# The first chunk of a gated-delta stage in another order: key transposes and two unread products first, value rows last, and the second inverse sent from another queue

## What is computed

```python
def gdn_chunk(S, xs):
    q, k, v, g, beta = xs
    ...
    a_mat = jnp.where(strict, beta[..., :, None] * jnp.einsum('bhid,bhjd->bhij', k, k) * decay, 0.0)
    lmat = a_mat + jnp.eye(c, dtype=F32)
    rhs = jnp.concatenate([beta[..., None] * v, (beta * jnp.exp(G))[..., None] * k], axis=-1)
    sol = lax.linalg.triangular_solve(lmat, rhs, left_side=True, lower=True, unit_diagonal=True)
    u, w = sol[..., :DV_A], sol[..., DV_A:]
    v_new = u - jnp.einsum('bhck,bhkv->bhcv', w, S)
    qk = jnp.einsum('bhid,bhjd->bhij', q, k) * decay
    o = jnp.einsum('bhck,bhkv->bhcv', q * jnp.exp(G)[..., None], S) + jnp.einsum('bhij,bhjv->bhiv', qk, v_new)
    ...
```

```python
def sb_sample(q, k_new, v_new, cache_k, cache_v, page_table, bias):
    ...
    return (jnp.einsum('bhqk,bkhd->bqhd', a[..., :past], vp)
            + jnp.einsum('bhqk,bkhd->bqhd', a[..., past:], v_new))
```

## Time and profile before

| | us |
|---|---|
| median of 3 runs | 1370.7 (1368.13 to 1372.23) |
| the profiled execution | 1375.66 |
| its span in the trace | 1373.6 |
| PE busy | 1321.5 (96%) |
| DVE busy | 800.4 (58%) |
| ACT busy | 524.5 (38%) |
| POOL busy | 177.4 (13%) |

### The profile page before, as it was taken

How to read it: one execution, slowest core, us unless ns; L and a number is a source line. 1 busy time by engine, 2 the same in 40 slices (tenths; PEclk the granted TensorE clock), 3 DMA queues, 4 the chain that set the end, 5 groups by cost and what they waited for, 6 DMA issues and landing times.

```text
span 1373.6 us, 27802 instructions
## 1 busy us (share of the span) xinstructions
PE 1321.5 (96%) x10527; PEld 1217.2 (89%) x10527; DVE 800.4 (58%) x2973; ACT 524.5 (38%) x794; POOL 177.4 (13%) x252
## 2 busy tenths in 40 slices
PE   6999999998999899999999999999999999999998
PEld 5999976787799787878988788999999999999998
DVE  5688759967989947886574223345544444433222
ACT  4333357635855422334325332234422222222222
POOL 1000001100720352400310000001211111110000
PEclk9999999999999969999999999999999999999999
DMA  8559968759733289989879986423333333332232
GB/s 307 175 177 321 329 205 299 262 189 333 232 100 101 67 278 331 366 293 308 240 232 344 370 280 200 139 78 92 90 94 93 92 94 92 94 88 87 85 100 74
DMA packets 256859, 265.56 MB, mean 193 GB/s; under 512 B 22987, under 2 KB 215677, under 8 KB 255927
## 3 DMA queue, kind: packets, MB, share of 16 engines
q1 hardware_dynamic: 256295, 262.75, 59.1%
q10 hardware_dynamic: 432, 1.06, 0.2%
HBM read 244.26 MB, written 19.70 MB: 192 GB/s over the span
## 4 chain that ended last, share of the span: by engine, by line
PE 70%; DVE 10%; DMA 6%; SPq 6%; ACT 4%; issue 3%; POOL 2%; POOLq 0%; ACTq 0%; DVEq 0%
PE ps L1178 51%; DMA wring<-in_w_in 3%; PE ps L1216 3%; PE ps L1290 3%; SPq L781 2%; DVE kring L2405 2%; DVE R L2486 2%; PE ps L1301 1%; DVE wring_split L646 1%; PE ps L1275 1%; PE ps L1475 1%; PE ps L1492 1%; SPq L847 1%; POOL R L3061 1%; SPq L784 1%
## 5 line engine op out<-in xcount | busy, mean ns | idle before, releaser
L1178 PE MATMUL ps<-obT_split,wring_split 128*128 128x268 f32 (+2 forms) x1296 | 263.2, 284 | 0.0
L1178 PE MATMUL ps<-obT_split,qv_split 128*128 128x260 f32 (+2 forms) x1024 | 214.1, 290 | 5.0 <-DVE wring_split L646 3.4
L646 DVE TENSOR_TENSOR wring_split<-wring,vring_split 128x1024 fp32r<-128x1024 f32 (+1 forms) x92 | 118.7, 1291 | 149.3 <-ACT vring_split L640 149.2
L1178 PEld LDWEIGHTS ps<-obT_split,wring_split 128*128 128x128 f32 (+1 forms) x1296 | 200.2, 187 | 0.5
L1178 PE MATMUL ps<-obT_split,vring_split 128*128 128x260 f32 (+1 forms) x960 | 195.8, 285 | 0.7 <-issue 0.7
L1178 PE MATMUL ps<-xn_split,vring_split 128*128 128x260 f32 (+1 forms) x960 | 193.2, 282 | 0.0
L1178 PE MATMUL ps<-xn_split,qv_split 128*128 128x260 f32 (+2 forms) x896 | 182.1, 285 | 0.0
L1178 PEld LDWEIGHTS ps<-obT_split,qv_split 128*128 128x128 f32 (+1 forms) x1024 | 157.7, 188 | 21.7 <-issue 18.1
L1178 PEld LDWEIGHTS ps<-obT_split,vring_split 128*128 128x128 f32 x960 | 147.7, 188 | 3.2 <-issue 2.9
L1178 PEld LDWEIGHTS ps<-xn_split,vring_split 128*128 128x128 f32 x960 | 148.0, 188 | 0.1
L640 ACT ACTIVATE vring_split<-wring 128x1024 fp32r<-128x1024 f32 (+1 forms) x92 | 95.2, 1036 | 132.3 <-DMA wring<-in_w_ffn_out 84.3
(11 more groups left out here) (424 smaller groups left out, 2111.8 us busy)
## 6 DMA issues: line engine op xcount, KB each, us to landing
wring<-in_w_in SPq DMA_DIRECT2D x72, 512.0 KB, 6.7
kring<-in_cache_k SPq DMA_DIRECT2D x64, 512.0 KB, 5.6
wring<-in_w_ffn_in SPq DMA_DIRECT2D x44, 512.0 KB, 3.7
vring<-in_cache_v SPq DMA_DIRECT2D x32, 512.0 KB, 5.8
kring<-in_cache_v SPq DMA_DIRECT2D x32, 512.0 KB, 5.8
vring<-in_cache_k SPq DMA_DIRECT2D x24, 512.0 KB, 5.6
R<-in_cache_k SPq DMA_DIRECT2D x24, 512.0 KB, 6.7
obT<-in_cache_v SPq DMA_DIRECT2D x24, 512.0 KB, 6.0
```

Source lines behind the costliest of these rows:

```text
L646: nc.vector.tensor_tensor(fr(w_part(wlo[:, p % RING, :], p)), w_part(wring[:, p % RING, :], p), w_part(w_high(p), p), ALU.subtract).then_i ...
L1178: last = mm(ps[0:m, tile_bank(t) + i, 0:n], fr(w), fr(x[k][:, a + i * n:a + i * n + n]), start=(k == 0 and w is w_h and x is hi), stop=(k ...
```

## The change

Five edits, all in the opening of the chunk stage:

- On PE, `key_rows(0)` stands first, then two new products `ones x cT` of 128x512, whose result nothing reads, then level 32 of chunk 0. `level_first(1, 32)` and V quad 4 stand ahead of `value_rows(0)`, and `sampled_norm` behind quad 5.
- `value_rows(0)` goes into bank pair 0 instead of pair 3. It therefore waits for DVE's level 64 of chunk 0, and quad 4 waits for `kr` instead of `bv`.
- The 8 transfers of `get_inverse(1)` leave SP's list and are sent by ACT (`second_inverse`) behind the norm rows, ahead of tile 23. They wait for POOL's zeros.
- On POOL, `zero_inverse(1)` moves ahead of the copy for tile 23, and the mask of level 32 of chunk 1 ahead of `decay_columns(0)`.
- On DVE, level 64 of chunk 0 stands ahead of the sampled tokens' convolution (`conv_sampled`).

```diff
-HEAD_PAIR = {("q1", 32): 2, "tk": 3, ("up", 32): 0, ("q1", 64): 2, ("up", 64): 0, "tv": 3, "kq": 2}
+HEAD_PAIR = {("q1", 32): 2, "tk": 3, ("up", 32): 0, ("q1", 64): 2, ("up", 64): 0, "tv": 0, "kq": 2}
...
                     chunk_pages(0, 3)
-                    get_inverse(1)
                     decay_columns(1)
...
                     elif n == QUADS:
-                        pe.wait_ge(g_dve, DVE_AT[0, "bv", 1])
+                        pe.wait_ge(g_dve, DVE_AT[0, "kr", 1])
...
+                key_rows(0)
+                for i in range(2):
+                    mm(ps[:, 4 + i, :], ones[:, :], cT[:, H, 0:512], start=True, stop=True)
                 level_first(0, 32)
-                key_rows(0)
                 level_second(0, 32)
...
-                value_rows(0)
...
+                level_first(1, 32)
+                early_quad(0, 0)
+                value_rows(0)
                 for c in range(TT):
...
+            def second_inverse():
+
+                act.wait_ge(x_out, 32)
+                act.wait_ge(tu_zero, 4)
+                for blk in range(4):
+                    o, r = 32 * blk, 32 + 8 * blk
+                    for i, buf in ((0, Tm[1]), (1, Um[1])):
+                        act.dma_start(buf[o:o + 32, :, o:o + 32],
+                                      xdram[i][r:r + 8, :].rearrange("h (i j) -> i h j", j=32))\
+                           .then_inc(inv_state_in[1], 16)
...
                             q_rows()
+                            second_inverse()
...
                 conv(NQKV - 1)
+                level_64(0)
                 conv_sampled()
-                level_64(0)
...
                     g_.memset(even(QL, 32), 0.0).then_inc(g_pool, 1)
+                    pool.wait_ge(x_out, 32)
+                    zero_inverse(1)
...
             level_mask(0, 64)
+            level_mask(1, 32)
             decay_columns(0)
-            pool.wait_ge(x_out, 32)
-            zero_inverse(1)
-            level_mask(1, 32)
             level_mask(1, 64)
```

More of the change, by code:

```diff
@@ L714, in level_32 @@
             return [(c, (n, 32), g) for g in G2 for n in ("U", "T")] if LEVELS.get(c) else []
-        pe_keys = level(0, "q1", 32) + both(0, "tk") + level(0, "up", 32) + level(0, "q1", 64)
-        pe_keys += level(0, "up", 64) + both(0, "tv")
+        pe_keys = both(0, "tk") + level(0, "q1", 32) + level(0, "up", 32) + level(0, "q1", 64)
+        pe_keys += level(0, "up", 64) + level(1, "q1", 32) + both(0, "tv")
         act_keys = level(0, "q1", 32) + level(0, "q1", 64) + both(0, "dc")
@@ L720, in build @@
         pool_keys = level(0, "L", 32) + [(0, "zq")] + level(0, "L", 64)
-        pool_keys += both(0, "df", "cm") + level(1, "L", 32) + level(1, "L", 64)
+        pool_keys += level(1, "L", 32) + both(0, "df", "cm") + level(1, "L", 64)
         for c in range(TT):
@@ L724, in build @@
             more = d < TT
-            pe_keys += (both(c, "ks") if c else []) + level(d, "q1", 32) + (both(c - 1, "ot") if c else [])
+            pe_keys += (both(c, "ks") + level(d, "q1", 32) + both(c - 1, "ot")) if c else []
             pe_keys += both(c, "vn") + level(d, "up", 32) + both(c, "qs" if c else "kq") + both(c, "kv")
@@ L1435, in value_rows @@
                             pe.wait_ge(cs_done, 2 * H + 4 * g + 4)
-                            after("dve", 0, "kr", g)
-                        elif LEVELS[c]:
+                        if LEVELS[c]:
                             after("dve", c, ("U", 64), g)
@@ L1576, in chunks @@
                         state_products(c, "ks")
-                    level_first(d, 32)
-                    if not c:
-                        sampled_norm()
-                    early_quad(c, 0)
-                    if c:
+                        level_first(d, 32)
+                        early_quad(c, 0)
                         outputs(c - 1)
@@ L1587, in chunks @@
                     early_quad(c, 1)
+                    if not c:
+                        sampled_norm()
                     level_second(d, 32)
```

## The result

The changed kernel takes 1374.22 us (median of 16 runs, 1366.96 to 1382.62), the kernel before 1370.87 in the same comparison (16 runs, 1367.19 to 1374.63). The ratio is 1.0035, interval 1.0021 to 1.0049: slower by 3.4 us, just beyond what can be told from no change, where 1364.2 and "faster" were forecast. The profiled execution took 1382.62 us (span 1380.8), the longest of the 16, so its profile shows what can happen in the changed kernel and not its median.

The account below looks back on a forecast made before the run. PE's narrow steps at half clock bound the opening, then quad 5's pages. Against the median, 1370.7 - 7.3 = 1363.4; half of a 1.5 us clock fall added gave 1364.2 us, range 1361.0 to 1370.5.

Parts of the forecast that it names:

- The prize: Chunk stage's opening, 477.61 to 502.40: 24.8 us of PE's small steps, about 12.4 at the full clock.
- Transposes and products: Start of the chunk stage: they fill PE's idle stretch, level 32 starts at 478.95, net cost 0.35 us, clock should hold.
- the agreement that the prediction saw: Clock 0.50 at 500 behind the value rows' eight transposes, agreeing with the rule that transposes don't count as busy.
- The second inverse on ACT: Opening: ACT sends eight transfers in 4 us (bounds 5.07, 7.21); PE waits 0.4 to 0.5 us for the level copy.
- The slower rival: Opening: ACT's transfers hold the level copy, PE idles 3.7 us, clock falls; 1375.0, decided from about 7 us sending; chance 0.07.
- The rest of the opening and quad 4: Level 32's second step to quad 4: quad 4 starts about 490.6 instead of 502.40, 11.8 us earlier.
- DVE before new values: Behind quad 4: new values wait for `bv`, start at 494.2, end at 496.1; PE idles 0.8 us.
- Quad 5's data: Quad 5's pages: landing at 498.5, between 495.4 and 500.5; PE idles 2.4 us.
- The norm behind quad 5: Uncovered ACT roots and copy: level 32's second step at 502.2 to 502.3 instead of 509.56, gain 7.3 us.
- the clock falls at quad 5's wait and stays down: Rival: from quad 5's wait through level 32's narrow steps at low clock; gain 2.3 us, 1368.4; chance 0.27.
- What follows: Behind quad 5: SP's list (quads 6, 7, third inverse) 7.7 us earlier; nothing later takes the 7.3 back.
- the prediction's own signs of being wrong: ACT sends for over 5 us, `bv` late by over 2 us, or PE waits later for pages now in time.

Follow-up runs that it names:

- b_again1: The kernel before, unchanged, profiled once more; 1370.81 us.
- b_again2: The kernel before, unchanged, a further profiled execution; 1370.10 us.
- e1: The kernel before with only chunk 0's key transposes and the two unread products put first in the chunk stage; 1370.78 us, ratio 1.0000.
- e6: The changed kernel with SP sending the second inverse right behind the first, and the sampled norm ahead of quad 5; 1372.42 us, ratio 1.0020.
- e15: The kernel before with SP's early second inverse, POOL's zeros early, key rows and two products first, norm ahead of quad 5; 1372.26 us, ratio 1.0024.
- e8: The kernel before with SP sending the second inverse right behind the first and POOL's zeros early; 1369.92 us, ratio 0.9984, in a repeat 1.0014.
- e10: The kernel before with the sampled norm behind quad 5 instead of ahead of quad 4; 1376.45 us, ratio 1.0048.
- e2: The changed kernel without the two unread products; 1375.59 us, ratio 1.0060.
- e9: e6 without the two unread products; 1371.76 us, ratio 1.0003.
- a_again: The changed kernel, unaltered, one more profiled execution; 1386.47 us.
- e4: The changed kernel with the sampled norm back ahead of quad 4; 1377.38 us, ratio 1.0055.
- e5: The changed kernel with SP sending nothing of the chunk stage until ACT's eight transfers have landed; 1379.74 us, one run.
- e7: The changed kernel with the sampled norm behind the new values, ahead of quad 5; ACT still sends the second inverse; 1370.78 us, ratio 1.0002.
- e12: e7 with DVE's sampled convolution ahead of its level 64, as in the kernel before; 1371.09 us, ratio 0.9993.
- e3: The changed kernel with the second inverse sent by SP right behind the first, instead of by ACT; 1375.03 us, ratio 1.0035.
- e13: The kernel before with the sampled norm behind quad 5 and two unread 128x512 products behind the norm; 1371.08 us, ratio 1.0011.

## Why the prediction was wrong

**The prize.** "From 477.61 to 502.40 are 24.8 us; at the full clock they would be about 12.4. That is the prize." The reading was right for that execution, but the kernel also opens in another way, without this prize, and both further profiles of it did (b_again1 and b_again2, 1370.81 and 1370.10 us, near the median). The text saw that the profile stood 5 us above the median and still took the whole gain off the median. By its own steps, level 32's second step was to start at 502.2, which is 26.4 behind the last tile. Against 33.8 in the profile read that is 7.3 us; against 28.4 in b_again1 it is 2.0. This is the step that failed first: the sum should have been taken against both.

**Transposes and products.** As forecast: 1.09 and 1.88 us modelled, level 32 at 476.76, and the clock 1.00 at 476. The clock holds in e1, but its profile had the short opening, in which it holds with nothing changed. The better evidence is in e6 and e15: there the clock was 1.00 up to the last tile, as in before, e8 and e10, but with the key transposes and products first PE idled 0.44 and 0.46 us and the clock stayed at 1.00 through level 32. The transposes and the window around them in e6:

```profile
472.76 1.09 PE L1427 MATMUL ps<-ident,R 128*128 128x128 f32 x8 [0.44 <-DVE dz L2458]
...
460.00:480.00 20.00, 17.36 (x135) 16.03 (x134) 18.23 (x29) 6.09 (x11) 13.61 (x13) 1.00 0.41 108
```

So this step seems to do what was forecast, in one of the two openings; the medians (e1, ratio 1.0000) do not show it. The Trainium skill, page "TensorE: Matmul & The Clock Gate", Part 4, says that transposes do not count as busy for the clock gate as other products do. No run here tests this alone: in e2 and e9, with the transposes and no products, the clock had fallen ahead of the last tile. Nor does the agreement that the prediction saw hold, since the clock had stood at 0.50 since 478 when the value rows' transposes ran.

**The second inverse on ACT.** 4 us were taken, with 5.07 and 7.21 as bounds. Measured: 3.86 to 3.88 in five profiles, 6.00 and 5.68 beside SP's pages in the two of the changed kernel itself. In the profile after ACT also began 1.1 us behind the last tile instead of 0.4 ahead of it, since POOL's zeros had been reckoned from POOL's row and the tile's end from PE's, and the two shift against each other between executions: the zeros ended 1.1 us behind the tile in after and a_again, 1.8 to 1.9 ahead of it in e2, e4, e5, e7 and e12. 2.0 and 1.5 more, and 0.45 of wait forecast, give 3.95; PE waited 4.08. The slower rival had this mechanism, but its point of decision (7 us) was put too high by that shift. It is seen in both profiles of the changed kernel, which are its longest runs. It is still not what makes the median slower: with it possible e7 takes 1.0002, and without it e3 takes the same 1.0035. That this rival's 1375.0 lies near the measured 1374.2 is chance.

**The rest of the opening and quad 4.** Forecast at 490.6, 14.8 behind the tile. Where PE did not wait for ACT, it was there: 13.9, 15.1, 15.8 in e7, e3, e5. In the profile after it was at 27.0, all narrow steps at half clock.

**DVE before new values.** Forecast `bv` at 494.2, 18.4 behind the tile, with 3.85 us for the sampled part. In e7 that part took 8.2 us (from 487.28 to 495.5), and PE got `bv` at 21.8. The 3.85 was taken from a stretch in which POOL was done after the first operation (1.42 us in the earlier trace rows); the others of its kind ran alone. PE then had the new values at half clock, and quad 5 started at 25.9, 3.2 us later than forecast. In e7, the changed kernel but for the norm, this is what takes the 2.0 us left above: level 32's second step starts at 27.9, against 28.4 in b_again1.

**Quad 5's data.** Forecast to land at 498.5, 22.7 behind the tile. Where ACT sends the inverse and began ahead of the tile's end, it was right: the last page landed at 22.9, 23.0, 23.2 and 23.6 in e7, e4, e12 and e2, against 25.1 in before and b_again1. In after and a_again, where ACT began later, it landed at 25.3 and 24.9, and PE came later still. The prediction had set beside it the rule of the Trainium skill, page "Trainium Kernel Development and Optimization", section Key Constraints, that several senders save only issue time on the same 16 engines; by that alone the landing was to be 500.5, 24.7 behind the tile. The four landings are 1.1 to 1.8 us earlier than this, so the measurement sides with the forecast. Only where SP sends the inverse ahead of quad 4 (e9, e3, e6: pages at 25.0, 25.2, 26.7), or is held back (e5: 25.9), does PE wait for the pages.

**The norm behind quad 5.** Forecast: a wait of 1.6 us at 26 behind the tile. Measured: 1.54 to 1.55 in every kernel with that order. Its price was put at 0.75 us, half of the cost of a stretch of 3 us at half clock, and no row of the prediction shows such a stretch (the shortest in the traces is 3.4 us); this was the second failed step. The fall lasts 6.8 us in after, e2, e3 and e10, which costs 3.4, and with the wait quad 5 to quad 6 is 5.2 us longer than in e1. The rival "the clock falls at quad 5's wait and stays down" came close: it had the fall, and the narrow steps that stay slow behind it, but counted from the gain of 7.3 us that was not there. It also put most of the blame on quad 5's wait, while e10 shows it without any.

**What follows.** SP's list was to be 7.7 us earlier. It sends quad 6 at 509.32 instead of 506.51, 35.6 behind the tile instead of 30.7, and 25.5 in b_again1 (501.36). Behind quad 6 the rest of the stage takes 112.1 us in after and 112.4 in before, so nothing is given back or lost there. Over all profiles this rest varies from 108.7 to 115.8 us, more than the whole effect, so the column "end" of one profile decides nothing; e3 and e6 end at the same place though quad 6 is 2.4 us apart.

**The sum after the runs.** The opening gives nothing that can be measured (e1, e7, e9). The norm's place costs 0.48% on the kernel before, clear of noise (e10), and 0.33% by the ratios on the changed one (after against e7, intervals that overlap). That is as much as the whole result, 0.35%. Two of the prediction's own signs of being wrong came true: ACT sent for more than 5 us in the two profiles of the changed kernel, and `bv` was late by more than 2 us (3.4 in e7). The first is not what the median shows; the second is why the opening gains nothing in e7. Open is why e10's runs have so low a clock on the whole: the median of their mean clocks is 0.981, in e13 0.987. Over 1376 us this is some 17 us more at half clock. Its profile has 6.8 behind the norm, and 27.3 instead of 10.2 in an opening like that of the profile before, ahead of anything that the edit moves; whether the order has a part in how often this happens was not tried. The stretch from quad 5 to quad 6 accounts for 3.2 of the 5.4 us between e10 and e13; the rest is not explained.

## What to carry to other kernels

A prize read from one execution must be found in a second before it enters the sum (seven profiles of this opening fell into two kinds), above all where it hangs on the clock. Before a small step is moved out from under a long one, ask what answer PE needs from the other engine: 1.5 us uncovered cost 5 us here, and two products that nobody reads, or one quad behind the step, took the loss away. An early part of a stage was worth nothing here while later inputs (pages, `bv`, the norm's squares) set the point where the next part starts.

## What the runs showed of the hardware

- The same eight transfers of 32 KB take ACT 3.86 to 3.88 us to send (e2, e4, e5, e7, e12), and 5.68 to 6.00 while SP sends four of 512 KB (a_again, after). In the chain after, one of them takes 1.69 us, others 0.35.
- DVE's operations on two SBUF inputs slow down beside POOL. In e7, DVE and POOL:

```profile
488.68 1.34 DVE L2512 TENSOR_TENSOR qv<-cbuf,convw 128x192 f32<-128x192 f32 x1
490.05 1.29 DVE L2514 TENSOR_TENSOR R<-R,qv 128x192 f32<-128x192 f32 x1
```

```profile
487.16 5.31 POOL L3093 TENSOR_TENSOR kring<-R,lvl 128x512 f32<-128x512 f32 x4
```

  The same two take 0.41 and 0.36 us where POOL rests (before, 494.63 and 495.07). The Trainium skill, page "SBUF — State Buffer", section "SBUF: two separate sides", says that such an operation and a GpSimd operation that reads SBUF lock each other out for a whole instruction; 1.3 us is one of POOL's four, and the trace agrees.
- The clock's fall does not follow from a wait's length alone in what it costs. Behind 2.68 and 3.24 us in e9, each followed by a quad, the half clock lasted 3.4 us. Behind 1.54 us in e10, followed by narrow products, it lasted 6.8, and behind 4.08 us in after, with narrow products until quad 4, 20.5.
